# First feed-forward layer of a two-block transformer kernel: modulation parts brought in by quarters and multiplied chunk by chunk, parameter rows and the rotary table moved to the eighth pair

## The chip, the cores and the metric

The kernel runs on one core of a Trainium2 chip. The metric is the device time of one execution in microseconds (us); smaller is better. Of three timed runs of the kernel before the median counts.

## The reference

Two stacks of layers run over 256 tokens of width 1024, all in float32. The first stack has two layers, each with three parts (feed-forward, token mixing, feed-forward), and each part's input is normed, scaled and shifted by vectors that come from a conditioning vector `c`. Only its head matters here:

```
cond = jax.nn.silu(c)
for l in range(DEPTH):                                    # DEPTH = 2
    mod = cond @ ada_w[l] + ada_b[l]                      # 1024 x 9216
    sh1, sc1, g1, sh2, sc2, g2, sh3, sc3, g3 = jnp.split(mod, 9, axis=-1)
    h = rms_norm(x, norm_ffn1[l]) * (1.0 + sc1) + sh1
    x = x + 0.5 * (1.0 + g1) * ((silu(h @ ffn1_w1[l]) * (h @ ffn1_w3[l])) @ ffn1_w2[l])
    ...
```

`ffn1_w1` and `ffn1_w3` are 1024 x 2816, `ffn1_w2` is 2816 x 1024. The second stack (four layers of attention or convolution mixers and feed-forward) stays as it is.

## The kernel before

**Weights.** All weights pass through SBUF once, as a list of *units*: 1024 rows by 256 columns, 1 MB each, laid as 8 chunks of 128 rows. SyncE issues their transfers in the list's order into four buffers `raw0` to `raw3` (`sync_program`); a buffer is loaded again once its unit has been read. A float32 product is built from two parts of each operand: ScalarE copies a unit's rounded high part into one of three `wsp` buffers (`ready_act`), VectorE subtracts it from the raw values for the low part (`ready_dve`), and TensorE multiplies high by high, high by low and low by high. A `wsp` buffer is free again when the unit three before has been multiplied. Each engine's program is written out by hand in `tensor_program`, `scalar_program`, `vector_program`, `pool_program` and `sync_program`; semaphores join them.

**Modulation.** `ada_w` is 36 units per layer; unit j gives 256 values of `mod`, that is 2 columns of the tile `MOD`. Units 0 to 7 hold the shift and the scale of the first part (`part_of` says which is which). Half of these eight are *fresh*: TensorE multiplies them straight from `raw` as float32, 32 products of one column each (`ada_pe`; the profile counts 64 instructions). The others, and all later ones, are reduced by VectorE with eight instructions over the 8 chunks into `ACC` (`ada_step`), and TensorE then sums the partitions in 4 products (8 instructions). `mod_dve` adds the bias, and after the last unit of a scale it makes the scale tile `AB`. After the eighth unit the list goes on with the feed-forward units, an `ada` unit between them here and there (`plan_ffn`).

**The opening.** ScalarE's queue fetches parameter rows 0 to 2 and GpSimd's queue rows 3 to 5 (biases, norm gains, convolution taps; 128 rows of 128 values each, `rows_dma`). TensorE turns rows 0, then x in 8 chunks, then rows 1 and 2. Then come the eight `ada` units, the sums of squares (`sums_pe`) and the spread of the root over partitions (`spread_pe`). `norm_dve` and `norm_act` build the normed input `HX`, high and low part, in four quarters of two chunks, and the pairs of the first feed-forward layer start.

**A pair.** `ffn_pe`, `ffn_act` and `ffn_dve` go over 11 pairs of units (`f1`, i) and (`f3`, i): multiply both, add the halves, silu, product, split into `FG`. TensorE's results go to PSUM, 8 banks in 4 pairs P0 to P3. `take` and `take2` hand out the banks longest free, and `give` attaches to them the marks that the next user has to wait for. Ahead of the fourth pair (`i == 3 and f == 0`) TensorE turns parameter rows 3 to 5 into three banks, VectorE computes the rotary angles (`rope_dve`), ScalarE takes their sine and cosine (`rope_act`) and only after that copies the turned rows out of the banks (`turned_act`).

**The other way to enter a layer** is in the kernel already, for parts n = 1 to 5 (`early(n)`, `lins_early`, `high_act`, `low_dve`, `scaled`): x times the scale, without the norm, is split into `XB` with the shift as two more columns (258 in all), multiplied as it is, and the root and the shift's product are applied to the result. Each chunk takes three products of 258 columns instead of one of 512 and one of 256.

`mark` and `AMOD`, `AMM`, `ARED`, `HLO`, `PCA` in the code are counters; `wait_ge` on them is skipped where the engine already knows the value.

**Lines.** In the profile an instruction has the line of the method of `Eng` that issued it: L66 `matmul`, L69 `transpose`, L72 `activation`, L75 `tensor_tensor`, L80 `tensor_scalar`, L83 `scalar_tensor_tensor`, L95 `tensor_copy`, L98 `reciprocal`, L104 `dma_start`. The functions named above stand at L208 (`part_of`), L225 (`plan_ffn`), L360 and L375 (`ready_act`, `ready_dve`), L439 and L446 (`take`, `take2`), L657 (`rows_dma`), L724 (`rope_dve`), L769 (`ada_pe`), L942 and L967 (`norm_act`, `norm_dve`), L1016, L1071 and L1126 (`ffn_pe`, `ffn_act`, `ffn_dve`).

## Time and profile before

| | |
|---|---|
| median of three runs | 2802.19 us (2797.94 to 2802.31) |
| the profiled execution, its own time | 2800.25 us |
| its span, first to last instruction | 2798.4 us |
| TensorE busy | 2747.1 us, 98% |
| VectorE busy | 2094.7 us, 75% |
| ScalarE busy | 1480.9 us, 53% |
| chain that ended last, TensorE's share | 91% |
| DMA | 521.44 MB, mean 186 GB/s |

The page divides the span into 40 slices of 70 us. TensorE is at 90% or more in all but the first, where it is at 60%. Everything that the change touches lies in the first 250 us. A time in a row is counted from the first instruction. A number after x is how many instructions a row holds; a duration in a row runs from the first's start to the last's end.

### The profile page before, as it was taken

The numbers are of one execution on the slowest core, as the hardware profiler recorded it, in microseconds if no ns is written. First come the engines' busy times: TensorE is split into PE (matmuls) and PEld (weight loads), VectorE is DVE, ScalarE is ACT, GpSimd is POOL, SyncE is SP. The second block draws the span as 40 slices with busy tenths as digits, with TensorE's granted clock in tenths as the row PEclk, the third lists the DMA queues.
The fourth block names the chain that finished last, engine by engine and source line by source line (L and its number), as shares of the span: only waits on it lengthen the run. The fifth ranks groups of instructions, "written<-read, shape, count | busy, mean of one in ns | idle before, by whom it ended". The sixth has DMA issues, their size and how long they took to land.

```text
span 2798.4 us, 53534 instructions
## 1 busy us (share of the span) xinstructions
PE 2747.1 (98%) x22658; PEld 2460.5 (88%) x22658; DVE 2094.7 (75%) x3300; ACT 1480.9 (53%) x2030; POOL 138.4 (5%) x257
## 2 busy tenths in 40 slices
PE   6999999999999999999999999999999999999999
PEld 6888899998888898998988988889888988898888
DVE  7987767789878877677886687755776677668874
ACT  3545754665455467446554466544654455436653
POOL 1000000200000000002000040000100000004000
PEclk9999999999999999999999999999999999999999
DMA  9775327548768752474685525555465557551553
GB/s 310 250 253 181 110 93 241 182 151 269 261 208 270 255 168 93 136 224 155 195 274 183 182 76 181 185 177 181 134 198 181 183 172 230 183 184 63 184 189 109
DMA packets 517006, 521.44 MB, mean 186 GB/s; under 512 B 16551, under 2 KB 513776, under 8 KB 516768
## 3 DMA queue, kind: packets, MB, share of 16 engines
q1 hardware_dynamic: 514160, 517.32, 57.5%
q8 instruction: 179, 2.93, 0.4%
q0 software_dynamic: 816, 0.27, 0.1%
q10 hardware_dynamic: 1792, 0.44, 0.1%
q14 instruction: 59, 0.48, 0.0%
HBM read 516.94 MB, written 1.05 MB: 185 GB/s over the span
## 4 chain that ended last, share of the span: by engine, by line
PE 91%; DVE 5%; ACT 2%; issue 1%; DMA 1%; POOL 0%; ACTq 0%; DVEq 0%
PE P L66 89%; PE P L69 2%; DVE wsp L75 1%; DVE arena L83 1%; ACT wsp L72 1%; DVE arena L75 1%; ACT arena L72 1%; DVE ACC L83 0%; DVE HX L83 0%; DMA raw<-in_ada_w 0%; DMA arena<-in_norm_ffn 0%; POOL arena L80 0%; DVE arena L89 0%; DVE X L95 0%; ACT HX L72 0%
## 5 line engine op out<-in xcount | busy, mean ns | idle before, releaser
L66 PE MATMUL P<-HX,wsp 128*128 128x512 f32 (+1 forms) x9920 | 1531.2, 315 | 10.4 <-DVE wsp L75 5.3
L66 PEld LDWEIGHTS P<-HX,wsp 128*128 128x128 f32 x9920 | 1381.1, 190 | 141.1 <-issue 12.6
L75 DVE TENSOR_TENSOR wsp<-raw,wsp 128x2048 fp32r<-128x2048 f32 (+4 forms) x454 | 947.3, 2090 | 282.4 <-ACT wsp L72 281.3
L72 ACT ACTIVATE wsp<-raw 128x2048 fp32r<-128x2048 f32 (+4 forms) x454 | 793.5, 1750 | 475.5 <-PE P L66 401.2
L66 PE MATMUL P<-FG,wsp 128*128 128x256 f32 (+1 forms) x2816 | 497.0, 337 | 0.0
L66 PEld LDWEIGHTS P<-FG,wsp 128*128 128x128 f32 x2816 | 428.4, 188 | 63.3 <-DVE wsp L75 1.2
L72 ACT ACTIVATE arena<-P 128x512 f32<-128x512 f32 (+3 forms) x375 | 208.3, 571 | 476.6 <-PE P L66 452.0
L75 DVE TENSOR_TENSOR arena<-arena,P 128x512 f32<-128x512 f32 (+2 forms) x226 | 147.0, 652 | 160.4 <-ACT arena L72 135.9
L83 DVE SCALAR_TENSOR_TENSOR ACC<-raw,sm,ACC 128x256 f32<-128x256 f32 x476 | 230.9, 485 | 16.8
L66 PE MATMUL P<-GX,wsp 128*128 128x256 f32 (+1 forms) x1592 | 229.3, 303 | 0.8 <-DVE GX L75 0.8
L66 PEld LDWEIGHTS P<-GX,wsp 128*128 128x128 f32 x1592 | 209.9, 190 | 14.2 <-issue 1.5
L66 PE MATMUL P<-arena 64*64 64x64 f32 (+9 forms) x4064 | 211.5, 258 | 9.6 <-issue 5.9
L66 PEld LDWEIGHTS P<-arena 64*64 64x64 f32 (+3 forms) x4064 | 166.8, 143 | 51.2 <-issue 23.1
L80 POOL TENSOR_SCALAR arena<-arena,sm 128x128 f32<-128x128 f32 x192 | 91.3, 486 | 1231.8 <-DVE sm L98 1229.9
L72 ACT ACTIVATE arena<-arena 128x512 f32<-128x512 f32 (+2 forms) x174 | 105.6, 614 | 29.3 <-DVE arena L75 19.0
L72 ACT ACTIVATE FG<-arena 128x512 fp32r<-128x512 f32 x88 | 55.7, 633 | 105.3 <-DVE arena L75 105.1
L72 ACT ACTIVATE arena<-arena,sm 128x128 f32<-128x128 f32 (+1 forms) x206 | 92.0, 451 | 27.1 <-DVE sm L89 26.5
L75 DVE TENSOR_TENSOR arena<-arena 128x512 f32<-128x512 f32 x144 | 98.8, 690 | 7.8 <-ACT arena L72 3.4
L72 ACT ACT_TABLE_LOAD x62 | 79.5, 1283 | 17.1 <-issue 10.3
L83 DVE SCALAR_TENSOR_TENSOR arena<-arena,PC 128x256 f32<-128x256 f32 x160 | 74.2, 483 | 3.4
L69 PE MATMUL P<-C,arena 128*128 128x128 f32 x410 | 63.2, 287 | 12.4 <-DMA arena<-in_norm_ffn 10.8
L89 DVE CUSTOM_DVE_ANT_0 arena<-P,C 128x128 f32<-128x128 f32 x192 | 59.8, 352 | 17.1 <-PE P L66 16.8
(119 smaller groups left out, 1490.7 us busy)
## 6 DMA issues: line engine op xcount, KB each, us to landing
raw<-in_ffn_w SPq DMA_DIRECT2D x120, 1024.0 KB, 5.4
raw<-in_ada_w SPq DMA_DIRECT2D x72, 1024.0 KB, 5.1
raw<-in_w_in SPq DMA_DIRECT2D x52, 1024.0 KB, 5.2
raw<-in_ffn_w_gate SPq DMA_DIRECT2D x44, 1024.0 KB, 5.4
raw<-in_ffn_w_up SPq DMA_DIRECT2D x44, 1024.0 KB, 5.3
raw<-in_ffn_w_down SPq DMA_DIRECT2D x32, 1024.0 KB, 4.9
raw<-in_nsa_w_in SPq DMA_DIRECT2D x20, 1024.0 KB, 5.4
raw<-in_ffn_w SPq DMA_DIRECT2D x16, 768.0 KB, 4.2
```

The source lines that it names most:

```text
L66: return self if self.e is None else self.e.matmul(*a, skip_group_check=True, **k)
L69: return self if self.e is None else self.e.transpose(*a)
L72: return self if self.e is None else self.e.activation(*a, **k)
L75: return self if self.e is None else self.e.tensor_tensor(*a)
L80: return self.e.tensor_scalar(o, a, s1, None, op0) if op1 is None else self.e.tensor_scalar(o, a, s1, s2, op0, op1)
L83: return self if self.e is None else self.e.scalar_tensor_tensor(out=o, in0=a, scalar=s, in1=b, op0=op0, op1=op1)
L89: return self.e.tensor_tensor_reduce(o, a, b, scale, 3.0e38, ALU.add, ALU.min, least)
```

## The change

It rewrites the way into the first part (n = 0) and the places of some small work:

- `part_of` and `fresh`: the eight first `ada` units come as scale quarter 0, shift quarter 0, scale quarter 1 and so on. Scale quarters are the reduced ones, shift quarters the fresh ones.
- The list of units: two `ada` units, the first pair of feed-forward units, the other six `ada` units, the second pair. Pairs 2 to 10 get their `ada` units at other places; by the end of the layer the count is the same, 20.
- Part 0 is entered by `XB` (`early(n)` now holds for n = 0), and the first three pairs multiply `XB`; `norm_dve` and `norm_act` run after the second pair and `HX` is used from the fourth on.
- `first_pe`, `first_act`, `first_dve`: four rounds. In round q the two chunks of quarter q are multiplied for both units, and among those of the second unit stands the fresh product of the next shift quarter.
- Parameter rows 0 go on SyncE's queue ahead of the weights. Rows 1 to 5, the positions and two small vectors go on GpSimd's queue, after the last `ada` unit of the eight.
- Rows 1 to 5 are turned, and the rotary table is made, at `i == 7` instead of 3.

```diff
         def part_of(j):
             x = j % 36
+            if j < 8:
+                return j // 2 if j % 2 else 4 + j // 2
...
-            return j < 8 and j % 2 == 0
+            return j < 8 and j % 2 == 1
...
-                if ada and (i in (2, 3, 4, 6, 7, 8, 10) if f else i % 4 != 3 and i < 10):
+                if f == i == 0:
+                    plan_ada(6)
+                elif ada and (i in (2, 3, 4, 6, 7, 8, 10) if f else i in (2, 4, 5, 6, 8, 9, 10)):
                     plan_ada(1)
...
-                    if ada and (s == 0 or f and s == 2 and q == 0):
+                    if ada and (s == 0 or s == 2 and q == 0):
...
-        plan_ada(8)
+        plan_ada(2)
...
         def start_act(e):
-            for t in range(3):
-                rows_dma(e, t)
...
-            for t in (1, 2):
-                turned_act(e, t)
...
         def start_pool(e):
+            e.wait_ge(*AMOD.at(7))
...
-            for t in range(3, nrow):
+            for t in range(1, nrow):
                 rows_dma(e, t)
...
         def early(n):
-            return 1 <= n < 6
+            return n < 6
...
+        def first_dve(e):
+            u = U["f1", 0][0]
+            for q in range(4):
+                ready_dve(e, U["ada"][2 * q], U["ada"][2 * q])
+                mod_dve(e, 2 * q)
+                low_dve(e, 0, q)
+                if q == 0:
+                    square_dve(e, 0, 1)
+                    square_dve(e, 0, 2)
+                mod_dve(e, 2 * q + 1)
+                if q == 0:
+                    ready_dve(e, u, u)
+                shift_pair_dve(e, q)
+                if q == 0:
+                    ready_dve(e, u, u + 1)
+                    root_dve(e, 0)
+            ready_dve(e, U["ada"][7], U["f1", 0][1])
+
+        def first_pe(e):
+            us = [U["f1", 0][0], U["f3", 0][0]]
+            ada_pe(e, 0)
+            ada_pe(e, 1)
+            sums_pe(e, 0)
+            ps = [take2(e, (k, 0, 0)) for k in ("f1", "f3")]
+            for q in range(4):
+                chunks = (2 * q, 2 * q + 1)
+                chunks_early(e, us[0], ps[0], 0, chunks)
+                if q < 3:
+                    b = take(e, ("ada", 2 * q + 3))
+                    chunks_early(e, us[1], ps[1], 0, chunks, lambda i: fresh_pe(e, 2 * q + 3, b, i // 2, range(4 * (i % 2), 4 * (i % 2) + 4)))
+                    give(("ada", 2 * q + 3), AMOD.at(2 * q + 3))
+                    ada_pe(e, 2 * q + 2)
+                else:
+                    chunks_early(e, us[1], ps[1], 0, chunks)
+                if q == 0:
+                    spread_pe(e, 0)
...
         def ffn_pe(e, f, n):
             for i in range(NB):
-                if i == 3 and f == 0:
-                    for t in range(3, nrow):
+                if i == 7 and f == 0:
+                    for t in range(1, nrow):
                         turn_rows(e, t)
...
+                        if n == 0 and i < 3:
+                            chunks_early(e, u, p, 0, range(8))
...
         def ffn_act(e, f, n):
             for i in range(NB):
-                if i == 3 and f == 0:
+                if i == 7 and f == 0:
                     rope_act(e)
-                    for t in range(3, nrow):
+                    for t in range(1, nrow):
                         turned_act(e, t)
...
+                if f == 0 and i == 1:
+                    norm_act(e, 0, U["f3", f][i])
```

**How the order moves: TensorE, the way into the first pair.** `sm` with `raw` is a fresh product (`sm` holds silu of c), `ACC` the sum behind a reduced unit, `HX` or `XB` a product with a weight unit in `wsp`. Before, from the last units on:

```order
L66 MATMUL P3<-sm,raw0 64x1 [waits raw0_landed,x_added]
L66 MATMUL P3<-sm,raw0 64x1 x31
L66 MATMUL P0<-C,ACC1 64x1 [waits ada_reduced,x_added]
L66 MATMUL P0<-C,ACC1 64x1 x3
L69 MATMUL P0<-C,sm 128x128 [waits norm_recip,cols_copied]
...
L66 MATMUL P1<-sm,raw2 64x1 [waits raw2_landed,cols_copied]
L66 MATMUL P1<-sm,raw2 64x1 x31
L66 MATMUL P1<-C,ACC0 64x1 [waits ada_reduced,mod_added]
...
L66 MATMUL P2<-C,ACC1 64x1 [waits ada_reduced,norm_root]
...
L66 MATMUL P3<-HX,wsp0 128x512 [waits h_lo,mod_added,weights_lo]
```

Now, the second round (the third reads the same, from `raw1`):

```order
L66 MATMUL P2<-XB_52,wsp0 128x258 [waits h_lo]
L66 MATMUL P2<-XB_52,wsp0 128x258 x11
L66 MATMUL P3<-XB_52,wsp1 128x258 [waits norm_root]
L66 MATMUL P3<-XB_52,wsp1 128x258 x2
L66 MATMUL P1<-sm,raw3 64x1 [waits raw3_landed]
L66 MATMUL P1<-sm,raw3 64x1 x7
L66 MATMUL P3<-XB_52,wsp1 128x258 x3
L66 MATMUL P1<-sm,raw3 64x1 x8
...
L66 MATMUL P0<-C,ACC0 64x1 [waits ada_reduced,mod_added]
L66 MATMUL P0<-C,ACC0 64x1 x3
```

Before, every `ada` unit stood ahead of the first weight product. Now a round is 24 products with `XB` and a fresh unit among them, then one `ACC` sum, and the next round's first product waits for `h_lo`, which VectorE makes from that sum.

**TensorE, where the rows are turned.** Before, ahead of the fourth pair (`C,ACC` is the `ada` sum, the L69 rows turn the parameter rows; the first product of each later unit follows, P is its pair of banks):

```order
L66 MATMUL P0<-HX,wsp2 128x512 [waits weights_lo,gate_sum]
...
L66 MATMUL P2<-C,ACC0 64x1 [waits ada_reduced,mod_added]
...
L69 MATMUL P3<-C,arena_49 128x128 [waits rows3_landed,up_sum]
L69 MATMUL P3<-C,arena_49 128x128 [waits rows4_landed]
L69 MATMUL P2<-C,arena_49 128x128 [waits rows5_landed,mod_added]
L66 MATMUL P1<-HX,wsp0 128x512 [waits weights_lo,gate_sum]
...
L66 MATMUL P0<-HX,wsp1 128x512 [waits weights_lo,up_sum]
...
L66 MATMUL P3<-HX,wsp2 128x512 [waits weights_lo,cols_copied]
```

Now, ahead of the eighth pair:

```order
L66 MATMUL P2<-HX,wsp1 128x512 [waits weights_lo,gate_sum]
...
L66 MATMUL P1<-C,ACC1 64x1 [waits ada_reduced,mod_added]
...
L69 MATMUL P3<-C,arena_49 128x128 [waits rows1_landed,up_sum]
L69 MATMUL P3<-C,arena_49 128x128 [waits rows2_landed]
L69 MATMUL P1<-C,arena_49 128x128 [waits rows3_landed,mod_added]
L69 MATMUL P0<-C,arena_49 128x128 [waits rows4_landed,gate_sum]
L69 MATMUL P0<-C,arena_49 128x128 [waits rows5_landed]
L66 MATMUL P2<-HX,wsp2 128x512 [waits weights_lo,up_sum]
...
L66 MATMUL P3<-HX,wsp0 128x512 [waits weights_lo,cols_copied]
...
L66 MATMUL P1<-HX,wsp1 128x512 [waits weights_lo,cols_copied,mod_added]
```

Before, the three turned rows lay in P3 and P2, the fourth pair's units took P1 and P0, and the wait for copied rows (`cols_copied`) stood at the third unit after the turns. Now five rows lie in P3, P1 and P0. The unit after the turns takes P2, which the unit just before the turns has filled, and the wait for copied rows stands at the second.

## Rows read from the trace of the kernel before

**Rows 1.** TensorE's waits, 0 to 200 us: us in total, times, longest.

```profile
PE P L66 <- DVE wsp L75: 0.5, 1, 0.5
```

**Rows 2.** Timeline, TensorE, opening: start, us, engine, line, operation, count, [idle before].

```profile
25.84 3.58 PE L66 MATMUL P<-sm,raw 128*64 128x1 f32 x64 [0.99 <-DMA raw<-in_ada_w]
...
38.81 0.59 PE L66 MATMUL P<-C,ACC 128*64 128x1 f32 x8 [3.01 <-DVE ACC L83]
44.13 12.71 PE L66 MATMUL P<-HX,wsp 128*128 128x512 f32 x64 [4.73 <-DVE HX L83]
...
57.10 11.42 PE L66 MATMUL P<-HX,wsp 128*128 128x512 f32 x64
```

**Rows 3.** Timeline, VectorE, opening.

```profile
11.79 3.41 DVE L95 COPY X<-P 128x256 f32<-128x256 f32 x8
...
18.97 3.61 DVE L83 SCALAR_TENSOR_TENSOR ACC<-raw,sm,ACC 128x256 f32<-128x256 f32 x7
...
39.62 2.29 DVE L75 TENSOR_TENSOR wsp<-raw,wsp 128x2048 fp32r<-128x2048 f32 x1
```

**Rows 4.** Timeline, ScalarE, opening.

```profile
37.67 1.91 ACT L72 ACTIVATE wsp<-raw 128x2048 fp32r<-128x2048 f32 x1 [16.36 <-DMA raw<-in_ffn_w]
40.61 1.91 ACT L72 ACTIVATE wsp<-raw 128x2048 fp32r<-128x2048 f32 x1 [1.02 <-DMA raw<-in_ffn_w]
```

**Rows 5.** DMA issues, 0 to 60 us: KB each, median us to landing.

```profile
arena<-in_x SPq DMA_DIRECT2D x1, 1024.0 KB, 5.1
```

**Rows 6.** Tile XB, whole span: ns min/median/max, first and last start.

```profile
L72 ACT ACTIVATE XB<-X,AB x40: 489/512/522, 191.5 to 1369.6; 128x256 fp32r<-128x256 f32 x40
L83 DVE SCALAR_TENSOR_TENSOR XB<-X,AB,XB x40: 474/485/490, 192.0 to 1370.2; 128x256 fp32r<-128x256 f32 x40
L72 ACT ACTIVATE XB<-MOD x5: 197/199/200, 237.6 to 1364.9; 128x16 fp32r<-128x16 f32 x5
```

**Rows 7.** Timeline, TensorE, a later entry by XB.

```profile
812.47 4.56 PE L66 MATMUL P<-XB,wsp 128*128 128x258 f32 x36
816.87 5.80 PE L66 MATMUL P<-HX,wsp 128*128 128x512 f32 x32
```

**Rows 8.** TensorE's groups by form, 44 to 46 us.

```profile
L66 PE MATMUL P<-HX,wsp 128*128 128x512 f32 x3 | 2.0, 673 | 4.7 <-DVE HX L83 4.7
```

**Rows 9.** TensorE's groups by form, 50 to 56 us.

```profile
L66 PE MATMUL P<-HX,wsp 128*128 128x512 f32 x19 | 6.2, 395 | 0.0
```

**Rows 10.** Timeline, TensorE, around 390 us.

```profile
382.93 6.01 PE L66 MATMUL P<-HX,wsp 128*128 128x256 f32 x48
388.87 2.03 PE L66 MATMUL P<-C,arena 128*64 128x1 f32 x64
390.83 11.34 PE L66 MATMUL P<-HX,wsp 128*128 128x256 f32 x80
```

**Rows 11.** Windows: length, busy of PE, PEld, DVE, ACT, POOL, granted clock, DMA.

```profile
44.00:46.00 2.00, 1.87 (x6) 1.61 (x7) 2.00 (x6) 1.33 (x4) 0.00 (x0) 1.00 1.11 389
393.00:394.00 1.00, 1.00 (x6) 1.00 (x6) 0.86 (x2) 1.00 (x1) 0.00 (x0) 0.50 0.00 0
```

**Rows 12.** Timeline, TensorE, third to fourth pair.

```profile
80.13 0.40 PE L66 MATMUL P<-C,ACC 128*64 128x1 f32 x8
80.46 0.55 PE L69 MATMUL P<-C,arena 128*128 128x128 f32 x3
...
92.59 0.59 PE L66 MATMUL P<-HX,wsp 128*128 128x512 f32 x2 [0.43 <-ACT PC L72]
```

**Rows 13.** Timeline, VectorE, fourth pair.

```profile
81.33 0.68 DVE L75 TENSOR_TENSOR arena<-arena,P 128x512 f32<-128x512 f32 x1
...
90.56 0.29 DVE L80 TENSOR_SCALAR arena<-arena 128x256 f32<-128x256 f32 x1
```

**Rows 14.** Timeline, ScalarE, fourth pair.

```profile
90.89 0.42 ACT L72 ACTIVATE ropec<-arena 128x256 f32<-128x256 f32 x1 [7.36 <-DVE arena L80]
...
92.07 0.59 ACT L72 ACTIVATE PC<-P 128x128 f32<-128x128 f32 x3
```

More of the change, by code:

```diff
@@ L658, in rows_dma @@
             st = ar(17152 + t * 128, 128)
-            e.wait_ge(*SET.at("rows"))
+            e.wait_ge(*SET.at("rows" if t else "row"))
             for base, c0, ap in prow[t][0]:
@@ L767, in fill_pe, with fresh_pe @@
                 ada_pe(e, nada[u])
+        def fresh_pe(e, j, b, q, ks):
+            u = U["ada"][j]
+            w = landed(u)
+            e.wait_ge(*RAW[u % NR].at(u))
+            e.wait_ge(*COND_.at("cond"))
+            for k in ks:
+                for x in range(2):
+                    ins = e.matmul(P[b][half(x), q:q + 1], w[:, k, 128 * q + 64 * x:128 * q + 64 * x + 64], COND[:, k:k + 1],
+                                   start=k == 0, stop=k == 7)
+            if q and ks[-1] == 7:
+                ins.then_inc(*AMM.up(j))
         def ada_pe(e, j):
@@ L772, in ada_pe @@
             if fresh(j):
-                w = landed(u)
-                e.wait_ge(*RAW[u % NR].at(u))
-                e.wait_ge(*COND_.at("cond"))
                 for q in range(2):
-                    for k in range(8):
-                        for x in range(2):
-                            ins = e.matmul(P[b][half(x), q:q + 1], w[:, k, 128 * q + 64 * x:128 * q + 64 * x + 64], COND[:, k:k + 1],
-                                           start=k == 0, stop=k == 7)
+                    fresh_pe(e, j, b, q, range(8))
             else:
@@ L811, in mod_dve @@
             q, w = x // 12, (x // 4) % 3
-            if x % 4 == 3 and w:
+            if j < 8 and w:
+                e.wait_ge(*AMOD.at(j))
+                c = 2 * (x - 4)
+                g = pcols["n10"] + c
+                e.scalar_tensor_tensor(ABS[0][:, c:c + 2], MODS[0][:, 8 + c:10 + c], 1.0, PC[:, g:g + 2],
+                                       ALU.add, ALU.mult).then_inc(*AMOD.up(("part", 0, 1, x - 4)))
+            elif x % 4 == 3 and w:
                 e.wait_ge(*AMOD.at(j))
@@ L826, in mod_ready @@
         def mod_ready(l, part):
-            return AMOD.at(36 * l + part_of(4 * part + 3)) if part % 3 == 0 else AMOD.at(("part", l, part))
+            if l == 0 and part < 2:
+                return AMOD.at(("part", 0, 1, 3) if part else 7)
+            return AMOD.at(36 * l + 4 * part + 7) if part % 3 == 0 else AMOD.at(("part", l, part))
         SQ = ar(0, 8, 256)
@@ L845, in early, with modulated @@
         def early(n):
-            return 1 <= n < 6
+            return n < 6
+        def modulated(n, part, q):
+            return AMOD.at(("part", 0, 1, q) if part else 2 * q + 1) if n == 0 else mod_ready(n // 3, 3 * (n % 3) + part)
         RE = ar(2048, 256)
@@ L889, in spread_pe @@
             ins.then_inc(*NSPR.up(n))
-            if n:
-                give(("nspr", n), NR_.at(n) if 0 < n < 14 else HT_.at((n, 3)))
+            give(("nspr", n), NR_.at(n) if n < 14 else HT_.at((n, 3)))
         def root_act(e, n):
@@ L945, in norm_act @@
                 root_act(e, n)
-            if early(n):
+            if early(n) and n:
                 e.wait_ge(*NSPR.at(n))
@@ L1035, in ffn_pe @@
                         p = take2(e, (k, f, i))
-                        if early(n) and i == 1 and k == "f1":
+                        if n == 0 and i < 3:
+                            chunks_early(e, u, p, 0, range(8))
+                        elif early(n) and i == (1 if n else 3) and k == "f1":
                             lins(e, [u], [p], HX, h_pairs(n))
@@ L1069, in unscaled_next, with begun_act, begun_dve, on_x @@
             return late(n + 1) or early(n + 1)
+        def begun_act(e, f, i, u):
+            if f or i:
+                ready_act(e, u)
+            else:
+                ready_act(e, U["ada"][7], U["f3", 0][1] if u == U["f1", 0][0] else None)
+        def begun_dve(e, f, i, u):
+            if f or i:
+                ready_dve(e, u)
+            else:
+                ready_dve(e, U["ada"][7], U["f3", 0][1] if u == U["f1", 0][0] else None)
+        def on_x(n, i):
+            return early(n) and i < (1 if n else 3)
         def ffn_act(e, f, n):
             for i in range(NB):
-                if i == 3 and f == 0:
+                if i == 7 and f == 0:
                     rope_act(e)
-                    for t in range(3, nrow):
+                    for t in range(1, nrow):
                         turned_act(e, t)
@@ L1134, in ffn_dve @@
             for i in range(NB):
-                if i == 3 and f == 0:
+                if i == 7 and f == 0:
                     rope_dve(e)
@@ L3173, in vector_program @@
             start_dve(e)
-            u = behind(-1)
-            for j in range(8):
-                mod_dve(e, j)
-                ready_dve(e, U["ada"][j], U["f1", 0][0] if j == 7 else U["ada"][7])
+            first_dve(e)
             for l in range(2):
-                norm_dve(e, 3 * l, u)
+                if l:
+                    norm_dve(e, 3 * l, u)
                 ffn_dve(e, 2 * l, 3 * l, (l, 0))
```

147 lines of the change are left out of this document (82 added, 65 removed).

## The prediction

> **What bounds the kernel now.** I read the page first: TensorE is busy 98% of the span, in all slices but the first. So a microsecond that TensorE idles or works longer stays in the result, and what the other engines do counts only where TensorE waits for it. The list of TensorE's waits and its timeline then give the few places, all in the first 200 us. The opening is one long wait for the norm's input: the last modulation sum ends at 39.4, the first wide product starts at 44.13 after 4.73 us of idling, the first pair is through at 56.8, and the second starts at 57.10 [rows 2]. From there TensorE runs pair after pair at 11.35 us plus 0.33 for an `ada` sum, with two small stops: 0.43 us for copied rows in the fifth pair [rows 12] and 0.5 us for a low part [rows 1]. **The start of the second pair, 57.10, is my mark**: all behind it is TensorE's own work plus stops. Behind the first layer the list of units is as before, so nothing there changes but its time.
>
> **TensorE has two prices.** In the opening a product of 512 columns shows a mean of 673 ns [rows 8], from 50 us on 395 [rows 9]: a factor of 1.7, though the granted clock reads 1.00 in both [rows 11]. Later the record shows the same thing openly: after 2 us of one-column products [rows 10] the granted clock stands at 0.50, that is 1.2 of 2.4 GHz [rows 11], and the 80 products around it take 11.3 us where 48 take 5.9 at full clock, so 1.4 us more than their 9.9 [rows 10]. The reading of 1.00 ahead of the first wide products is therefore not one I believe. TensorE was already busy with fresh products from before 25.84 on [rows 2] and the price stayed high; it fell only once wide ones ran.
>
> **The change, step by step** (us from the first instruction).
>
> *Start.* SyncE issues rows 0 behind x, five small transfers more ahead of the first unit, some 2 us by the earlier queues' spacing; cover: the queue is still moving x, which lands at 1.2 + 5.1 = 6.3 [rows 5]. Eight turned chunks cost VectorE 3.4 us [rows 3], with one copy more of at most that size 3.9, so it is free near 10.5. Transfers follow each other by 2.94 us [rows 4]; with 1 us for the small ones unit 0 lands at 10.2. The reduction takes 3.9 (started with one instruction of 0.35 ahead of the seven in [rows 3]) to 14.5, the sum 0.6 [rows 2] and the fresh unit 1 3.4 to 18.5. That frees the buffer of unit 3, the sixth in the list. Issued at 18.5 it could be there at 23.6 [rows 5], but the stream brings the sixth at 10.2 + 5 x 2.94 = 24.9, so 25.0. *Round 0* waits for it among its products.
>
> *A round* is 24 products with `XB`. One costs 0.122 at full clock: 36 in 4.40 us [rows 7]; 0.21 at the slow price. The fresh unit in it adds 3.4 [rows 2], a price seen only at the slow clock. So a round takes 6.3 to 8.4.
>
> *Between rounds* TensorE idles, since the chain is serial: the `ACC` sum 0.6 [rows 2], bias and scale on VectorE (two small ones, about 0.4, sized by the smallest of [rows 6]), two ScalarE copies 1.0, the second low part 0.5 [rows 6], the shift's bias, copy and low part 0.6, hand-overs 0.3: **3.4 us**. Three such links are on the path, and none in the old order, where all eight units were read before the first wide product.
>
> *Clock in the rounds.* Each round has about 5 us of wide work, half of it thinned by one-column products, and then 4 us of almost nothing. I take the slow price with 0.7 us off per round for a stretch at full clock. Round 0 ends at 25.0 + 5.3 = 30.3; with links and rounds of 7.7 the next start at 33.7, 44.8, 55.9; the last, without a fresh unit, takes 4.3 to 60.2. The second pair's first unit is split by then: ScalarE is free at 55.5, 1.9 for the high part [rows 4], 2.3 for the low [rows 3], 59.8. So the mark moves to 60.2, **+3.1**. Bounds: full clock throughout gives 56.2 (the split ends last), -0.9; the slow price throughout 62.4, +5.3.
>
> The Trainium skill, "TensorE: Matmul & The Clock Gate", section "Part 1: The HAM clock gate", says that the default is the throttled state and that activity releases it. By that rule every round starts at 1.2 GHz, which is the +5.3 end; the trace agrees in the 673 against 395 ns.
>
> *Transfers* after round 0 are early: a unit each 2.94 us from 25.0, while a round takes 11. The units of later rounds wait for TensorE and VectorE, not they for them.
>
> *Third and second pair by `XB`.* 48 products of 0.122 are 5.9 us a unit against 5.67: four units, **+0.8**. One `ada` sum that lay ahead of the mark is now behind it: **+0.3**.
>
> *The norm behind the second pair* adds 16 VectorE instructions, at 0.48 [rows 6] 7.8 us, and 8 on ScalarE. Cover: the first two pairs bring no reduction (3.9 each), and `HX` is asked for only by the fourth pair; its first quarter is there 4 us ahead by my count (the mark, 23.6 us of products, 0.3). Costed at nothing; if the cover were gone it would be at most those 4 us. `scaled` instead of the two-step copy costs nothing for the same reason.
>
> *GpSimd* now waits for the eighth modulation column and then issues some 35 transfers; behind the waiting instruction there is only that. Rows are needed 75 us later.
>
> *The eighth pair.* Call T the end of the seventh pair's products. The order shows three things. The unit after the turned rows takes P2, filled just before, so it waits for VectorE's add. Before, at the same place (T = 80.13 [rows 12]), this add ran 81.33 to 82.01 [rows 13], T + 1.9; TensorE could otherwise start at T + 0.6. **+1.3**. Then five rows occupy P3, P1 and P0, so the *second* unit after the turns waits for copied rows, where before it was the third. ScalarE copies them only behind sine and cosine, and those wait for VectorE's angles, which end at 90.85 [rows 13]; the first copies lie at 92.07 and the waiting product starts at 92.59 [rows 14, 12], T + 12.5. VectorE's queue at the eighth pair is the same, plus one scale (0.2): T + 12.7. TensorE has work until 1.9 + 5.7 = T + 7.6. It stands for **+5.1**. Before, 11.35 us of products lay in front of that wait and hid all but 0.43; now half of them do. After such a stop I expect one slow stretch, **+1.4** [rows 10]; bounds 0 and two of them, 2.8.
>
> The same page, section "HAM oscillation — how this bites in real kernels", warns against idle gaps in TensorE. By it the stop costs its length and a slow restart, 6.5 in all; without it 5.1.
>
> *Gone:* the stops of 0.43 and 0.5 [rows 12, 1], **-1.0** rounded up: VectorE gets ahead while TensorE stands.
>
> **Sum:** 3.1 + 0.8 + 0.3 + 1.3 + 5.1 + 1.4 - 1.0 = **+11.0**, with bounds +5.6 and +14.6. The profiled execution took 2800.25 us, 1.9 below the median of 2802.19; I add to the middle of the two, 2801.2, and get **2812.2**.
>
> **Rivals.**
>
> *A, the clock stays up.* If the mixed rounds hold full clock, the opening is -0.9 and no restart is paid: +5.6, 2806.8, at the very border of "slower". For it: the price fell once wide products ran. Against: each round has a fresh unit in its middle, and 2 us of one-column products brought the fall of [rows 10, 11]. 0.12.
>
> *B, the stop in the eighth pair is hidden.* If the copies of rows are done in time, 1.3 + 5.1 + 1.4 go: +3.2, 2804.4. It needs VectorE to reach the angles 5 us earlier, and by [rows 12 to 14] it is the chain and not a backlog that sets them: the last low part ahead of the angles waits for T itself. 0.11.
>
> *C, the other side: the rounds keep pace with the transfers.* If link and products of a round fitted into two landings (5.9 us), the last fresh unit's landing at about 37.5 would set the opening: 3.4 for it, one link, one last round, and the mark would come near 47, -10. With all else as in the sum that is -2.1: 2799.1, not slower; with B's relief as well -9.9. It decides where a round with its link drops below 5.9; I get 11.1, and 9.7 at full clock. 0.10.
>
> *D, more stops.* VectorE, which has the norm, the first `ada` reduction and two subtractions within the third pair, lets TensorE wait at the fourth pair too: up to 4 more, 2816. For it: those come to 7.8 + 3.9 + 4.6 = 16.3 us against 11.7 of a pair. Against: it enters that pair ahead. 0.10.
>
> My forecast has 0.57; its own range is 2807 to 2816.
>
> **Numbers.** The measurement of this kernel tells about 0.2% from no change, 5.6 us. Slower by more: the forecast, D and half of A, 0.73. Within: B, half of A, half of C, 0.22. Faster: 0.05, the half of C that has the stop hidden too. The range that leaves out about two in ten is 2804 to 2816.
>
> **What would show it.** In the profile after: TensorE's wide products start near 21, in four bursts with gaps of 3 to 4 us on `h_lo`; a gap on the DMA of an `ada` unit near 25; the second pair at 60; a wait of about 5 us for `PC` from ScalarE near 137, with the granted clock at 0.5 behind it; the wait of 4.73 us gone. I am wrong if the second pair starts before 56, if that wait is under 2 us, or if the rounds' gaps name DMA.

## The result, and the profile after

| | before | changed |
|---|---|---|
| median | 2802.24 us (2797.94 to 2802.31, 4 runs) | 2818.32 us (2815.63 to 2819.38, 4 runs) |
| profiled execution, its own time | 2800.25 us | 2818.40 us |
| its span | 2798.4 us | 2816.6 us |
| TensorE busy | 2747.1 us | 2762.0 us |

The ratio is 1.0061, with the interval 1.0049 to 1.0073: slower by 0.6%, 16 us. The forecast was 2812.2, with ranges of 2807 to 2816 and 2804 to 2816; the result lies above both. The direction and the places were right, the size was not.

TensorE's timeline of the changed kernel, which answers to [rows 2] (start, us, engine, line, operation, count, idle time before and its releaser):

```profile
15.08 0.59 PE L66 MATMUL P<-C,ACC 128*64 128x1 f32 x8 [4.51 <-DVE ACC L83]
21.85 3.56 PE L66 MATMUL P<-XB,wsp 128*128 128x258 f32 x15 [0.90 <-DVE XB L75]
26.00 1.02 PE L66 MATMUL P<-sm,raw 128*64 128x1 f32 x16 [0.58 <-DMA raw<-in_ada_w]
...
35.64 3.56 PE L66 MATMUL P<-XB,wsp 128*128 128x258 f32 x15 [1.90 <-DVE XB L75]
39.14 1.02 PE L66 MATMUL P<-sm,raw 128*64 128x1 f32 x16
40.09 1.01 PE L66 MATMUL P<-XB,wsp 128*128 128x258 f32 x3
...
45.69 0.57 PE L66 MATMUL P<-C,ACC 128*64 128x1 f32 x8
48.77 3.56 PE L66 MATMUL P<-XB,wsp 128*128 128x258 f32 x15 [2.51 <-DVE XB L75]
...
61.91 27.47 PE L66 MATMUL P<-XB,wsp 128*128 128x258 f32 x216 [2.51 <-DVE XB L75]
89.30 0.40 PE L66 MATMUL P<-C,ACC 128*64 128x1 f32 x8
89.63 22.65 PE L66 MATMUL P<-HX,wsp 128*128 128x512 f32 x128
```

The four rounds begin at 21.85, 35.64, 48.77 and 61.91. The first takes 13.79 us, with a wait for a transfer in it; the second and the third take 13.13, where 11.1 was forecast. The last row holds round 3 (24 products) and the next two pairs (192), which take 23.18 us elsewhere (the x192 row of e4_sum_first below, start to next start). So the second pair starts at 89.30 - 23.18 = **66.1**; before it was 57.10. There is no gap at 89.63, where rival D put its stop.

The windows of the same trace (length, TensorE's busy time and count, granted clock, DMA share and GB/s):

```profile
14.00:21.00 7.00, 5.87 (x104) 0.50 1.10 347
21.00:35.00 14.00, 11.31 (x98) 0.50 0.99 315
35.00:48.00 13.00, 10.62 (x96) 0.50 0.49 154
48.00:62.00 14.00, 10.71 (x97) 0.50 0.55 174
```

The first three rounds ran at 1.2 of 2.4 GHz throughout, though TensorE was busy for 77% to 84% of each window. The fourth starts so (62 to 65 us reads 0.50) and rises within. Its 24 products took 4.2 us (27.39 to the next start, less 23.18). The DMA share falls to a half, and no gap behind the first round names a transfer: the transfers wait for the rounds, not the rounds for them.

The eighth pair, which answers to [rows 12]:

```profile
135.57 0.40 PE L66 MATMUL P<-C,ACC 128*64 128x1 f32 x8
135.90 0.76 PE L69 MATMUL P<-C,arena 128*128 128x128 f32 x5
137.11 5.84 PE L66 MATMUL P<-HX,wsp 128*128 128x512 f32 x32 [0.45 <-DVE arena L75]
147.90 19.64 PE L66 MATMUL P<-HX,wsp 128*128 128x512 f32 x96 [4.94 <-ACT PC L72]
167.47 0.40 PE L66 MATMUL P<-C,ACC 128*64 128x1 f32 x8
```

And ScalarE there, which answers to [rows 14]:

```profile
146.20 0.42 ACT L72 ACTIVATE ropec<-arena 128x256 f32<-128x256 f32 x1 [7.55 <-DVE arena L80]
...
147.37 0.93 ACT L72 ACTIVATE PC<-P 128x128 f32<-128x128 f32 x5
```

With T = 135.57 the second unit starts at T + 12.33, behind a wait of 4.94 us for rows that ScalarE copied at 147.37, after the table. The windows just behind it (busy time of PE, PEld, DVE, ACT and POOL, then the granted clock, DMA share and GB/s):

```profile
147.00:153.00 6.00, 5.10 (x16) 4.46 (x17) 3.67 (x4) 4.11 (x9) 0.00 (x0) 0.50 0.01 3
154.00:165.00 11.00, 11.00 (x65) 9.58 (x64) 8.16 (x12) 5.84 (x6) 0.00 (x0) 1.00 0.82 261
```

The 96 products from 147.90 on took 19.57 us to the next start. At full clock it is 16.91 (h1_fill below), so the half clock cost 2.7 here. In the other six profiles that have this stop the same products took 18.47 to 19.57 us, so it costs 1.6 to 2.7.

The first product of the layer's next part stood at 238.38 us before and stands at 256.21 now, and what lies behind is the same work. Even so, the profiled time less the start of this row runs from 2558.0 to 2562.8 us over the thirteen profiles of this case (2561.9 before, 2562.2 changed), so one execution can differ from another by up to 4.7 us in work that no edit touches. TensorE's rows there, before and changed:

```profile
238.38 3.85 PE L66 MATMUL P<-XB,wsp 128*128 128x258 f32 x30 [0.57 <-DVE XB L75]
```

```profile
256.21 3.85 PE L66 MATMUL P<-XB,wsp 128*128 128x258 f32 x30 [0.56 <-DVE XB L75]
```

That is +17.8 of the +18.15 between the profiled executions. It is made of 9.0 (the start of the second pair), 0.9 (the turned rows' bank), 4.9 (the wait for `PC`), 2.7 (the half clock behind it) and a rest of 0.3.

### The profile page after: what moved, and what is told of

It is laid out like the page before. It is cut to its first block, busy times and chain, and to the rows that moved or that the text cites. A ratio compares the mean times of both kernels' runs of the same rounds, so it can differ in the third digit from the quotient of the medians.

```text
span 2816.6 us, 53758 instructions
## 1 busy us (share of the span) xinstructions
PE 2762.0 (98%) x22754; PEld 2476.5 (88%) x22754; DVE 2099.7 (75%) x3325; ACT 1481.0 (53%) x2040; POOL 146.4 (5%) x273
## 3 DMA queue, kind: packets, MB, share of 16 engines
HBM read 516.94 MB, written 1.05 MB: 184 GB/s over the span
## 4 chain that ended last, share of the span: by engine, by line
PE 92%; DVE 4%; ACT 2%; issue 1%; DMA 0%; POOL 0%; DVEq 0%; SPq 0%; ACTq 0%
PE P L66 90%; PE P L69 2%; DVE arena L83 1%; DVE wsp L75 1%; ACT wsp L72 1%; ACT arena L72 1%; DVE arena L75 1%; DVE HX L83 0%; DMA raw<-in_ada_w 0%; DMA arena<-in_x 0%; POOL arena L80 0%; DVE ACC L83 0%; DVE arena L89 0%; DVE X L95 0%; ACT HX L72 0%
## 5 line engine op out<-in xcount | busy, mean ns | idle before, releaser
L66 PE MATMUL P<-HX,wsp 128*128 128x256 f32 (+3 forms) x9728 | 1496.9, 315 | 10.1 <-ACT PC L72 4.9
L66 PEld LDWEIGHTS P<-HX,wsp 128*128 128x128 f32 (+2 forms) x9728 | 1351.5, 190 | 137.0 <-issue 7.2
L66 PE MATMUL P<-XB,wsp 128*128 128x258 f32 x768 | 108.3, 301 | 9.5 <-DVE XB L75 9.5
L66 PEld LDWEIGHTS P<-XB,wsp 128*128 128x128 f32 x768 | 102.1, 204 | 11.2 <-DVE XB L75 7.4
L75 DVE TENSOR_TENSOR arena<-arena 128x512 f32<-128x512 f32 (+1 forms) x141 | 96.7, 689 | 5.7 <-ACT arena L72 1.4
```

Of the source, the lines that this page charges most:

```text
L66: return self if self.e is None else self.e.matmul(*a, skip_group_check=True, **k)
L75: return self if self.e is None else self.e.tensor_tensor(*a)
```

## The experiments

All start from the changed kernel unless said otherwise. Each ratio is to the kernel before, timed on the same chip beside it. The runs whose names begin with e and g were timed on one chip, in two sessions, and those with h on another.

### The eighth pair: copying before the sine

```diff
-                    rope_act(e)
                     for t in range(1, nrow):
                         turned_act(e, t)
+                    rope_act(e)
```

> The changed kernel with one thing swapped: in the eighth pair ScalarE copies the five turned rows out of their banks ahead of sine and cosine. Theory (the stop is a wait for banks): the 4.94 us wait of TensorE for PC goes, and with it the two slow clock windows behind it, 2.5 us; the second pair still starts at 66.3. Total 7.5 us below the changed kernel, near 2811. Rival (VectorE's 5.6 us of angles would stop TensorE anyway, by a late low part or a late add): the wait changes its name to a VectorE one of 3 to 5 us, total 2815 to 2818.

Measured: 2806.45 (2803.01 to 2810.57, 10 runs), ratio 1.0017 (1.0008 to 1.0027). TensorE's timeline of this kernel:

```profile
131.12 0.40 PE L66 MATMUL P<-C,ACC 128*64 128x1 f32 x8
131.45 0.76 PE L69 MATMUL P<-C,arena 128*128 128x128 f32 x5
132.66 22.58 PE L66 MATMUL P<-HX,wsp 128*128 128x512 f32 x128 [0.44 <-DVE arena L75]
```

ScalarE's copies of the turned rows, and its first step of the table:

```profile
134.10 0.93 ACT L72 ACTIVATE PC<-P 128x128 f32<-128x128 f32 x5
141.76 0.42 ACT L72 ACTIVATE ropec<-arena 128x256 f32<-128x256 f32 x1 [6.73 <-DVE arena L80]
```

The wait for `PC` is gone, both units run in one piece at full clock, and the 31.9 us from T to the next sum have become 24.05: the stop and its clock were worth 7.9 us. The gap of 0.44 for VectorE's add stays. With the rows at this place, it is the order of two steps on ScalarE that makes the stop. The kernel came out lower than the 2811 expected. In the profiled execution the opening, untouched by this edit, was shorter: its fourth round began at 57.45, not 61.91, and the second pair at 61.7, not at the 66.3 expected. That asked for repeats (below).

### The eighth pair with the old opening

The kernel before, with rows 1 to 5 turned and the table made at the eighth pair:

```diff
-                if i == 3 and f == 0:
-                    for t in range(3, nrow):
+                if i == 7 and f == 0:
+                    for t in range(1, nrow):
...
```

(and the same in `ffn_act` and `ffn_dve`; the turns and copies of rows 1 and 2 leave the opening.)

> The kernel before, with its own opening, but rows 1 to 5 turned and the rotary table made at the eighth pair, as the changed kernel does. Banks fall the same way as in the changed kernel. Theory (the eighth pair costs by itself): a wait of about 5 us for PC at the second unit behind the turns, granted clock 0.5 behind it for 3 to 7 us, the old stops of 0.43 and 0.5 us gone: 7 to 8 us above before, 2809 to 2810. Rival (the stop needs the state that the new opening leaves, VectorE late by it): no wait over 1 us, total 2802.

Measured: 2805.97 (2803.64 to 2808.10), ratio 1.0017 (1.0007 to 1.0026). Its timeline at that pair:

```profile
128.81 5.86 PE L66 MATMUL P<-HX,wsp 128*128 128x512 f32 x32 [0.45 <-DVE arena L75]
139.41 19.64 PE L66 MATMUL P<-HX,wsp 128*128 128x512 f32 x96 [4.74 <-ACT PC L72]
```

Bank, stop and slow 96 products are there without the new opening. At the next sum behind them this kernel was 8.3 us behind the kernel before (158.98 against 150.69), but the profiled executions differ by 5.7 and the medians by 4.8: the trace of before has three stretches at half clock between 200 and 2790 us, this one has one, and each is worth 1.4 [rows 10]. So the total is 3 to 4 us below the 2809 to 2810 expected, though the place behaved as the theory said. The rival, a wait that would vanish, is out.

### Fresh units in one piece

```diff
                     b = take(e, ("ada", 2 * q + 3))
-                    chunks_early(e, us[1], ps[1], 0, chunks, lambda i: fresh_pe(e, 2 * q + 3, b, i // 2, range(4 * (i % 2), 4 * (i % 2) + 4)))
+                    chunks_early(e, us[1], ps[1], 0, chunks)
+                    for h in range(2):
+                        fresh_pe(e, 2 * q + 3, b, h, range(8))
                     give(("ada", 2 * q + 3), AMOD.at(2 * q + 3))
                     ada_pe(e, 2 * q + 2)
```

> The changed kernel, but in each of the first three rounds all 24 wide products first, then the 32 one-column products of the fresh unit in one piece, then the sum. Theory A (switching between the two kinds costs, about 1.2 us a round, and the clock stays at half): rounds of 11.9 instead of 13.1 us, the first one 1.7 us shorter, second pair near 62.5, total 2814 to 2815. Theory B (5.6 us of wide products in one piece also bring the clock to full before the round ends): granted clock 1.00 in part of each block, second pair near 60, total 2811 to 2812. Rival (only the chain between rounds counts): nothing moves, 2818.

Measured: 2807.56 (2805.97 to 2809.53), ratio 1.0022 (1.0013 to 1.0031), 10.8 below the changed kernel's first median and below the lower of the two theories (2811 to 2812). Its ten runs all lie below the lowest of the changed kernel's thirteen (2811.34). One round of it:

```profile
32.33 5.50 PE L66 MATMUL P<-XB,wsp 128*128 128x258 f32 x24 [2.15 <-DVE XB L75]
37.76 2.21 PE L66 MATMUL P<-sm,raw 128*64 128x1 f32 x64
39.83 0.37 PE L66 MATMUL P<-C,ACC 128*64 128x1 f32 x8
42.73 5.50 PE L66 MATMUL P<-XB,wsp 128*128 128x258 f32 x24 [2.52 <-DVE XB L75]
```

and the window over it (columns as in the last windows):

```profile
35.00:48.00 13.00, 10.48 (x110) 10.13 (x108) 6.12 (x17) 1.12 (x3) 0.00 (x0) 0.63 0.61 190
```

A round is 10.4 us instead of 13.13, with the same work and a gap of 2.5. The 24 products still cost 0.23 each, the half-clock price, but the fresh unit behind them takes 2.1 where it took 3.7 in pieces: the granted clock rises just behind the wide block in each of the three rounds (near 28, 38 and 48 us). The second pair starts at 58.4. In the changed kernel's slow rounds mixing lost twice, by the clock and by the switching: at half clock 9 wide and 64 one-column products in turns took 6.55 (39.14 to 45.69 in the changed kernel), where 9 x 0.233 and 3.40 in one piece are 5.5. Mixed rounds can catch the full clock too, as the repeats below show, and then take 10.76.

### The sum ahead of the second unit

```diff
                 if q < 3:
                     b = take(e, ("ada", 2 * q + 3))
-                    chunks_early(e, us[1], ps[1], 0, chunks, lambda i: fresh_pe(e, 2 * q + 3, b, i // 2, range(4 * (i % 2), 4 * (i % 2) + 4)))
+                    for h in range(2):
+                        fresh_pe(e, 2 * q + 3, b, h, range(8))
                     give(("ada", 2 * q + 3), AMOD.at(2 * q + 3))
                     ada_pe(e, 2 * q + 2)
+                    chunks_early(e, us[1], ps[1], 0, chunks)
```

> The changed kernel, but in each of the first three rounds: 12 wide products of the first unit, the fresh unit in one piece, the sum, and only then the 12 wide products of the second unit. Theory (the rounds are long because the serial link of 3.1 us through ScalarE and VectorE starts after all products): the link now runs beside 2.8 us of products; rounds of about 9.6 instead of 13.1 us, next rounds near 33, 43 and 52, second pair near 58, total 8 us below the changed kernel, near 2810. Rival (rounds are TensorE work at half clock and the order inside them does not matter): gain no larger than that of the unmixed kernel, 3 to 4 us.

Measured: 2801.41 (2797.99 to 2803.43), ratio 0.9997 (0.9988 to 1.0006): 16.9 below the changed kernel, no difference from before, and nearly 9 below the 2810 expected. Its opening:

```profile
29.72 2.95 PE L66 MATMUL P<-XB,wsp 128*128 128x258 f32 x12
...
32.74 1.85 PE L66 MATMUL P<-XB,wsp 128*128 128x258 f32 x12
34.52 2.03 PE L66 MATMUL P<-sm,raw 128*64 128x1 f32 x64
36.41 0.48 PE L66 MATMUL P<-C,ACC 128*64 128x1 f32 x8
36.82 4.53 PE L66 MATMUL P<-XB,wsp 128*128 128x258 f32 x24
...
50.35 23.25 PE L66 MATMUL P<-XB,wsp 128*128 128x258 f32 x192 [0.64 <-DVE wsp L75]
73.53 0.40 PE L66 MATMUL P<-C,ACC 128*64 128x1 f32 x8
```

The chain from sum to the next `XB` now runs beside the second unit's 12 products, and no link shows a gap (g1_sum_copy, with the same opening, shows gaps of 0.88 and 0.25). The second pair starts at 50.35, 15.7 us earlier than in the changed kernel and 6.8 earlier than before. The three gaps (1.90, 2.51, 2.51) are 6.9 of that; the rest, which the expectation had not counted on, is the clock and the switching. The granted clock stood at 0.74 on average from 35 to 48 us and at 1.00 from 48 on, where the changed kernel had 0.50. It still fell twice, near 36.5 and 43.4 us, each time at the end of a fresh unit and its sum. The stop at the eighth pair (4.95) is as before the edit.

### Is it the clock? Work in the gaps

```diff
                     ada_pe(e, 2 * q + 2)
+                    b = take(e, ("dummy", q))
+                    wh = halves(us[1])[0]
+                    for i in range(12):
+                        s = slice(i % 2 * 128, i % 2 * 128 + 128)
+                        e.matmul(P[b][:, 0:258], wh[:, 2 * q, s], XB[:, 0, 2 * q, :], start=True, stop=True)
+                    give(("dummy", q))
```

> The changed kernel with 12 products of 258 columns more in each of the three links, behind the ACC sum, into a bank that nothing reads: TensorE works where it waited 2.5 us for the next quarter of XB. It leaves nothing out and computes more. Theory: the opening was 6.1 us longer than forecast because the granted clock stayed at 0.50 through all rounds, and it stays there because of the gaps and one-column products. Then the clock rises in some of the rounds although there is more work: rounds of 11 or less instead of 13.1, the mark 4 to 8 us earlier, the kernel at 2810 to 2815. Rival: the rounds are long by their chain and their work, whatever the clock: then 12 products of 0.233 are 2.8 us where 2.5 were idle, the rounds are 0.3 us longer and the kernel is at 2818 to 2820.

Measured: 2810.57 (2809.43 to 2811.90), ratio 1.0039 (1.0025 to 1.0053); the changed kernel beside it, 2817.44. The second round:

```profile
36.44 2.05 PE L66 MATMUL P<-XB,wsp 128*128 128x258 f32 x15
38.41 0.63 PE L66 MATMUL P<-sm,raw 128*64 128x1 f32 x16
38.98 0.62 PE L66 MATMUL P<-XB,wsp 128*128 128x258 f32 x3
...
42.25 0.38 PE L66 MATMUL P<-C,ACC 128*64 128x1 f32 x8
42.56 2.36 PE L66 MATMUL P<-XB,wsp 128*128 128x258 f32 x12
45.15 2.74 PE L66 MATMUL P<-XB,wsp 128*128 128x258 f32 x15 [0.23 <-DVE XB L75]
```

The kernel computes 36 products more and is 6.9 us faster. A mixed round at full clock takes 5.8 us (36.44 to 42.25), at half clock 10.05 (35.64 to 45.69). The rival, rounds that are long whatever the clock, is out. The second pair starts at 58.50, 7.5 us earlier than in the changed kernel timed beside it (g3_same_again below). All five runs lie below all five of that kernel. But the fill is not the only way to the full clock: the repeats below reach it for part of a round with the gaps in place.

### Is it the idling that halves the clock in the eighth pair?

```diff
                         else:
+                            if f == 0 and i == 7 and k == "f1":
+                                e.wait_ge(*LO.at(u))
+                                wh = halves(u)[0]
+                                for x in range(20):
+                                    e.matmul(v3(P[2 * p][:, :], 2), wh[:, x % 8, 0:128], HX[:, :, x % 8, :], start=True, stop=True)
                             lin_wide(e, u, p, HX).then_inc(*MM.up(u))
```

> The changed kernel with 20 products of 512 columns more in the eighth pair, put ahead of the first unit's own products into the same banks, which those then write anew. It computes more and leaves nothing out. At full clock they are 20 x 0.236 = 4.7 us (64 products of a pair take 11.35 us, a third of their columns being the narrow one's), just the length of the wait for PC. Theory: the wait is a date set by the chain of the table, 4.9 us, and the half clock behind it (2.55 us) comes from the idling. Then TensorE's wait shrinks to about 0.2, the products behind it end as early as without them, the two stretches at 0.50 are gone, and the kernel takes 2.5 us less: 2815. Rival 1: the granted clock falls there for another reason (the transposes and one-column products ahead of the pair): then the stretches stay and the time is 2817 to 2818. Rival 2: the chain to the table depends on the first unit's end: then the wait stays near 4.9 and the time rises by 2 to 4.7, to 2820 or more.

Measured: 2811.50 (2811.24 to 2814.70), ratio 1.0044 (1.0030 to 1.0058); the changed kernel beside it, 2812.35. Its eighth pair:

```profile
136.76 10.40 PE L66 MATMUL P<-HX,wsp 128*128 128x512 f32 x52 [0.45 <-DVE arena L75]
147.56 16.98 PE L66 MATMUL P<-HX,wsp 128*128 128x512 f32 x96 [0.41 <-ACT PC L72]
164.47 0.40 PE L66 MATMUL P<-C,ACC 128*64 128x1 f32 x8
```

The date of the second unit is the same (T + 12.33 there, 147.56 - 135.22 = T + 12.34 here): it is set by the chain of the table. But with TensorE at work until then, the 96 products take 16.91, not 19.57, and the granted clock stays at 1.00. The transposes and one-column products ahead of the pair are still there, so rival 1 is out: the slow stretch behind the stop comes from the idling. This rests on one profile of h1. In the medians it is not to be seen: they differ by 0.85 us, inside the spread of either, and not by the 2.5 expected. The two profiled executions took the same time, 2811.24 and 2811.34: in h1's the opening was 4.2 us longer (its rounds stayed at half clock), the 96 products were 1.9 shorter, and the untouched rest was 2.5 shorter.

### The changed kernel again, and the copy first again

> The changed kernel once more, beside the others on one chip, to see how far its own executions lie apart. In e1_copy_first the same opening ran 4.4 us shorter in the profiled execution, with two stretches at granted clock 1.00 that this kernel's profile does not have. If the clock in the rounds is a matter of the execution, the runs spread over some 4 to 7 us around 2814 to 2818 and a new profile may show the mark (start of the second pair) anywhere from 61 to 66. If the low clock belongs to the kernel, the runs lie within 2 us of 2818 and the mark is at 66 again.

> The changed kernel once more, for the spread of its opening. Both profiles so far have the granted clock at 0.50 from 13.8 to 65.0 us and the second pair at 66. I expect 2815 to 2818 again; a run below 2812 would show that its opening too can catch the full clock.

> The same kernel as e1_copy_first, beside the changed kernel of h3_same_third. Its opening is word for word that of the changed kernel, but its one profile showed rounds that rose to full clock twice. If the clock in the rounds falls differently from execution to execution, these runs spread from 2803 to 2811 as before (2817.9 less 7.4 for the wait and what follows it is 2810.5, the end with a half clock throughout), and a profile with the half clock throughout may turn up. If all runs lie at 2810 to 2811, the earlier profile was the exception.

Measured: g3 2817.44 (2814.99 to 2817.93, 5 runs), ratio 1.0061 (1.0048 to 1.0073); h3 2812.35 (2811.34 to 2814.47, 4 runs), ratio 1.0044 (1.0030 to 1.0058); h2 2810.46 (2803.18 to 2812.47, 5 runs), ratio 1.0032 (1.0019 to 1.0044). The profile of g3 has the rounds at 35.42, 48.55 and 61.68, all at half clock, like the first. That of h3 differs:

```profile
34.44 3.56 PE L66 MATMUL P<-XB,wsp 128*128 128x258 f32 x15 [1.90 <-DVE XB L75]
...
38.59 0.62 PE L66 MATMUL P<-XB,wsp 128*128 128x258 f32 x3
...
45.20 3.47 PE L66 MATMUL P<-XB,wsp 128*128 128x258 f32 x15 [2.51 <-DVE XB L75]
...
55.96 28.82 PE L66 MATMUL P<-XB,wsp 128*128 128x258 f32 x216 [2.51 <-DVE XB L75]
```

Its rounds are 10.76 apart, with a group in the alternating part taking 0.56 us where the clock is up, and not 0.95, and the windows over them (35 to 48 and 48 to 62 us) show a granted clock of 0.63 and 0.62. In six profiles of this same opening (the changed kernel three times, h1, e1, h2) the second and the third round are always one of two: 13.13 us, or 10.75 with a stretch at full clock in it. The first round, which also waits for a transfer, lies between 11.2 and 14.5. Which one comes differs even within one kernel: e1 and h2 are the same code, with rounds of 10.75, 10.75 in one profile and 10.77, 13.14 in the other, and its 15 runs reach from 2803.0 to 2812.5, over 7 us in either session. In h3's profile the fourth round begins 5.95 us earlier than in the first profile of the changed kernel, but it runs at half clock throughout, so the second pair starts at 61.5, 4.6 earlier. Its time is 7.1 less: 4.6 for that, 0.8 for the products behind the stop, 1.7 for the untouched rest.

Why one execution catches the full clock and another doesn't stays open. The five runs of g3 and the four of h3 do not overlap, and they were timed on different chips, so for this kernel the chip or the session is not ruled out as a part of it. And h2's median is only 1.9 below h3's, though in its profile the eighth pair is as short as in e1 (24.04 us from T to the next sum): what copying first is worth is read from the traces and from the next experiment, not from these two medians.

### Both edits together, and the old kernel with one of them

The edits of e4_sum_first and e1_copy_first in one kernel:

> The changed kernel with both edits tried apart: in each round the fresh unit and the ACC sum stand between the first unit's and the second unit's products, and in the eighth pair the turned rows are copied before the sine. If the two costs are separate and add, this is e4_sum_first less what the wait for PC is worth. That wait is 4.95 us in e4 and behind it one stretch at granted clock 0.50 (1.4 us), so 6.3 us less than its 2801.4: 2795.1, faster than both kernels, ratio to before 0.998. Rival: the stop only moves, to VectorE's queue or to a later pair, or a half-clock stretch appears elsewhere in the layer; then 2798 to 2801.

Measured: 2792.57 (2790.32 to 2795.99, 7 runs), ratio 0.9973 (0.9963 to 0.9984): faster than both kernels, by 6.7 us against before and 24.9 against the changed kernel beside it. The wait for `PC` is gone and nothing came in its place:

```profile
121.53 22.58 PE L66 MATMUL P<-HX,wsp 128*128 128x512 f32 x128 [0.45 <-DVE arena L75]
...
232.78 3.83 PE L66 MATMUL P<-XB,wsp 128*128 128x258 f32 x30 [0.57 <-DVE XB L75]
```

The next part starts at 232.78, 5.6 us earlier than before. Against e4_sum_first, which has the stop, the ratio to before fell from 0.9997 to 0.9973, that is by 6.7 us. The median is 2.5 below the 2795.1 expected; the rival, a stop that only moves, is out.

The kernel before, with the turned rows copied ahead of the sine at the fourth pair (the edit of e1_copy_first, at `range(3, nrow)`):

> The kernel before with one edit: ahead of the fourth pair ScalarE copies the three turned rows before it takes sine and cosine. It tells how much of the gain of copying first was open to the old kernel too. TensorE loses only the stop of 0.43 us: 2800.5 to 2801, no difference that can be measured. If copying first were worth more than the stop that TensorE shows (ScalarE and VectorE running ahead), it would come below 2799.

Measured: 2798.96 (2797.00 to 2801.76) against 2799.26, ratio 0.9997 (0.9988 to 1.0006). No difference, as expected: there 11.35 us of products hid all but 0.43 of the wait.

## Why the prediction was right and wrong, point by point

- **The step that failed is "Clock in the rounds".** Its mechanism was right and its size was not: the term +3.1 for the start of the second pair measured +9.0. It took 7.7 us for a round's work, between 6.3 and 8.4. Measured in the changed kernel: 10.05, at half clock throughout; at full clock it is 5.8 (g4_dummies). The upper end was too low for two reasons. A wide product at half clock costs 0.233 (15 in 3.50), not the 0.21 scaled from 0.122 by the factor 1.7 of [rows 8, 9]: +0.6 a round. And 9 wide products in turns with 64 one-column ones cost 1.05 more than apart. The rest is that I gave each round 0.7 us back for a stretch at full clock, and in this execution there was none. The lateness against the forecast starts of the rounds grows by that step: 1.9 us at the second round, 4.0 at the third, 6.0 at the fourth, and 5.9 at the second pair (66.1 against 60.2). What I called "the slow price throughout", +5.3, was +9.0, and even that with the fourth round partly at full clock.
- That bound was the place to see it: granted clock 0.50 was a case I named, and I scaled its price by the factor of 1.7 between two short windows with 3 and 19 products in them. The measured prices, 0.233 and 0.122, are a factor of 1.9 apart.
- *Start.* Unit 3's products at 26.0 (25.0 forecast), round 1 at 35.64 (33.7). First wide product 21.85.
- *Between rounds.* 3.08 us from the sum's start to the next product (3.4 forecast), 2.5 of it idle. Right, and the part of the loss that e4_sum_first took away whole.
- *Transfers* were early, as said: after the first round no wait names one.
- *Pairs by `XB`.* 192 products took 23.2 us (e4_sum_first), where [rows 2] has two pairs of 11.35: +0.5, not +0.8. With the moved sums and without the two old stops (0.43 and 0.54), the rest of the layer is +0.3, where the forecast had +0.1.
- *The norm's cover* held: no gap at the fourth pair. Rival D is out.
- *The eighth pair.* The bank cost 0.9 (1.3), the wait 4.94 (5.1), its date T + 12.33 (12.7). e1, e2 and h1 show its cause. The clock behind it cost 2.7, between the 1.4 taken and the bound of 2.8; in other executions down to 1.6.
- *Rival A* (the clock stays up) did not come by itself; g4_dummies shows what it would have been worth. *Rival B* was said to need VectorE's angles 5 us earlier. e1_copy_first shows another way: the copies do not depend on the angles, only on their place behind them in ScalarE's order. *Rival C* needed rounds of 5.9 with their link, and they took 13.1. Its landing at 37.5 does not follow from the rows either (25.0 + 4 x 2.94 = 36.8). e4_sum_first came near it, with its fresh units 8.7 and 6.8 us apart, and the second pair at 50.35 where C had 47.
- The forecast's 11.1 us a round is near what h3_same_third shows (10.76), and its median of 2812.35 is the predicted time. That is chance and doesn't make the step right: the kernel before stood at 2799.97 beside it, 1.2 below the base I added to, the rounds were 13.13 in two of three profiles of this kernel, and my range had no room for them.

## What to carry to other kernels

Where a serial chain links rounds of TensorE's work, put the producer of the next round's input (here a sum of 0.6 us) in the middle of the round, ahead of work that doesn't need it: this hid three gaps, went with a higher granted clock for much of the opening, and was worth 15.7 us there. Keep short one-column products in a block of their own (ten runs of e3_unmixed, all below the changed kernel's thirteen). And when a step is moved to another place, look for what its engine does first: in the trace, two steps of ScalarE in the other order took away 7.9 us that the move had cost. At the old place the same exchange made no difference (g2_before_copy), since enough products lay ahead of the wait.

## What the runs showed of the hardware

- In the changed kernel TensorE ran from 14 to 65 us at a granted clock of 0.50 while busy for about 80% of the time, in rounds of wide and one-column products with gaps of 1.9 and 2.5 us.
- The first records of a trace can read 1.00 though the price of a product is that of half clock: in e4_sum_first, which reads 1.00 up to 36 us, 12 products of 258 columns took 2.74 us from 29.72 on (0.228 each), against 0.121 later (192 in 23.18).
- Without gaps the clock could fall too: in e4_sum_first near 36.5 and 43.4 us, each time at the end of a block of one-column products.
- Thirty-six more products in the gaps made the same program 6.9 us faster (g4_dummies against g3_same_again, five runs each, side by side).
- Behind a stop of 4.7 to 4.9 us the same 96 products took 18.5 to 19.6 us in seven profiles; with TensorE kept at work until 0.4 us before them, 16.9 (h1_fill).
- One-column products are cheaper at full clock too: a fresh unit takes 3.40 us at half and 1.9 at full (e4_sum_first, 34.52 to 36.41).
- The clock can make two executions of one kernel differ by 2.4 us a round, in steps: in six profiles the second and third rounds of the same opening took 13.13 or 10.75 us and nothing between.
